# Neighbourhood attention: probabilities scaled on VectorE and plainly transposed, in place of products with a diagonal of 1/sum

## The reference, cut to what matters

```python
s = concatenate([s_nb + bias, s_cx], axis=-1)       # scores of one query
p = softmax(s.astype(float32), axis=-1)
o = einsum(p_nb, v_win) + einsum(p_cx, v_c)         # float32 throughout
```

## Time and profile before

| | us |
|---|---|
| executions | 4262.36, 4264.66, 4271.78 |
| median | 4264.66 |
| span of the profiled execution | 4259.6 |
| TensorE busy in the span | 3857.9 |
| VectorE busy | 1835.2 |
| ScalarE busy | 1324.2 |
| GpSimd busy | 456.7 |

### The profile page before, as it was taken

The page is one execution under the profiler, slowest core; times in us unless marked ns, Lnnn a source line. Parts: engine busy times, 40 slices in busy tenths (PEclk is TensorE's granted clock), DMA queues, the critical chain, the costliest instruction groups (busy, mean ns, idle before and its releaser), DMA issues.

```text
span 4259.6 us, 52528 instructions
## 1 busy us (share of the span) xinstructions
PE 3857.9 (91%) x21392; PEld 3013.5 (71%) x21392; DVE 1835.2 (43%) x2812; ACT 1324.2 (31%) x1963; POOL 456.7 (11%) x379
## 2 busy tenths in 40 slices
PE   7788878999998999899978889899998798989999
PEld 3555546788886787688865667678886566767887
DVE  2544443533334334444434354544333435454333
ACT  3332322322223323323333431233232333123222
POOL 0211110000002211000021230000011122000000
PEclk9878889999998999899989999999999999999999
DMA  4112243121111222232211221032321121113322
GB/s 162 53 48 80 90 170 108 50 70 60 60 53 57 80 95 85 74 102 92 89 46 34 68 57 40 30 106 90 99 85 41 43 74 50 33 39 108 96 93 69
DMA packets 320320, 317.03 MB, mean 74 GB/s; under 512 B 8720, under 2 KB 286128, under 8 KB 319952
## 3 DMA queue, kind: packets, MB, share of 16 engines
q1 hardware_dynamic: 320080, 313.67, 23.3%
HBM read 311.55 MB, written 2.10 MB: 74 GB/s over the span
## 4 chain that ended last, share of the span: by engine, by line
PE 78%; DVE 11%; ACT 5%; DMA 2%; issue 2%; POOL 1%; DVEq 0%; SPq 0%; ACTq 0%; POOLq 0%
PE PS L132 78%; DVE scr L146 5%; ACT scr L142 3%; DMA ring<-in_ada_w 1%; DVE scr L156 1%; DVE scr L164 1%; DVE PS L160 1%; ACT L142 1%; PE PS L135 1%; DVE NBt L156 1%; DVE scr L168 1%; POOL ring_r L146 1%; POOL NBt L146 0%; DVE scr L176 0%; DVE scr L152 0%
## 5 line engine op out<-in xcount | busy, mean ns | idle before, releaser
L132 PE MATMUL PS<-scr 128*32 128x32 f32 (+7 forms) x6692 | 648.1, 279 | 144.9 <-DVE scr L146 69.6
L132 PEld LDWEIGHTS PS<-scr 128*128 128x128 f32 (+4 forms) x6692 | 529.2, 167 | 291.2 <-issue 119.6
L132 PE MATMUL PS<-ffn_h,ffn_w 128*128 128x512 f32 (+1 forms) x3168 | 616.2, 357 | 7.8 <-DVE ffn_h L156 5.7
L132 PEld LDWEIGHTS PS<-ffn_h,ffn_w 128*128 128x128 f32 x3168 | 524.7, 190 | 100.5 <-issue 9.1
L142 ACT ACTIVATE scr<-PS 128x256 f32<-128x256 f32 (+5 forms) x425 | 193.2, 455 | 820.8 <-PE PS L132 752.6
L132 PE MATMUL PS<-h_h,ring_r 128*128 128x512 f32 (+1 forms) x976 | 356.6, 428 | 38.2 <-POOL ring_r L146 24.3
L142 ACT ACTIVATE scr<-scr 128x256 f32<-128x256 f32 (+7 forms) x404 | 212.6, 526 | 519.9 <-DVE scr L156 322.3
L132 PE MATMUL PS<-mlp_h,mlp_w 128*128 128x512 f32 x1536 | 361.3, 396 | 0.0
L132 PE MATMUL PS<-mlp_g,mlp_w 128*128 128x512 f32 x1536 | 359.7, 396 | 0.0
L132 PEld LDWEIGHTS PS<-mlp_h,mlp_w 128*128 128x128 f32 x1536 | 288.4, 188 | 70.5 <-issue 1.0
L132 PEld LDWEIGHTS PS<-mlp_g,mlp_w 128*128 128x128 f32 x1536 | 288.5, 188 | 69.9
(11 more groups left out here) (151 smaller groups left out, 4736.6 us busy)
## 6 DMA issues: line engine op xcount, KB each, us to landing
ring<-in_ada_w SPq DMA_DIRECT2D x48, 1024.0 KB, 6.1
ring<-in_ffn_w_in SPq DMA_DIRECT2D x44, 1024.0 KB, 5.0
ring<-in_w_up SPq DMA_DIRECT2D x32, 1024.0 KB, 5.5
ring<-in_w_down SPq DMA_DIRECT2D x32, 1024.0 KB, 5.0
ring<-in_w_in SPq DMA_DIRECT2D x60, 512.0 KB, 3.9
ring<-in_ffn_w_out SPq DMA_DIRECT2D x16, 1024.0 KB, 5.1
scr<-in_na_bias SPq DMA_DIRECT2D x32, 512.0 KB, 5.0
ring<-in_na_w_qkv SPq DMA_DIRECT2D x24, 512.0 KB, 4.2
```

The source lines that it names most:

```text
L132: return self.eng.matmul(o, lhsT=l, rhs=r, start=start, stop=stop) if self.eng else Nothing()
```

## The change

The diagonals go, and the buffer `dg` with them (the small buffers laid out behind it move up). VectorE takes the reciprocals of the sums as before and then scales `Pm` in place, one tensor-scalar operation of 128x512 per head, each with a count of its own. TensorE waits per head and transposes the four blocks of the head with the identity. The in-place scaling takes the place, on VectorE's queue, that the diagonal had: behind the reciprocal, ahead of the bias steps of the next item. The wait for the flip two items back, which protected `dg`, goes; ScalarE's own wait for that flip still protects `Pm`.

```diff
-    dg = [naa(256).rearrange("p (h t) -> p h t", h=2) for _ in range(2)]
@@ na_pe
         def flip(it):
             z = it % 2
-            pe.wait_ge(*at("n_dg", it))
             for hf in range(2):
+                pe.wait_ge(*at("n_sc", it, hf))
                 o = psum("n_pt", it, 1)[:, 512 * hf:512 * hf + 512]
                 for c in range(4):
-                    t = pe.mm(o[:, c * 128:c * 128 + 128], Pm[z][:, hf, c * 128:c * 128 + 128], dg[z][:, hf, :], True, True)
+                    t = pe.tr(o[:, c * 128:c * 128 + 128], Pm[z][:, hf, c * 128:c * 128 + 128], ident)
                 t.then_inc(*pe.up("nt_full", it, hf))
@@ na_dve
         def spread(it):
             z = it % 2
             dve.wait_ge(*at("n_ex", it))
-            dve.recip(nst[z][:, 4:6], nst[z][:, 4:6]).then_inc(*dve.up("n_dg"))
-            if it >= 2:
-                dve.wait_ge(*at("nt_full", it - 2, 1))
-            dve.tt(dg[z], bc(ident, 1, 2), bc(nst[z][:, 4:6], 2, 128), ALU.mult).then_inc(*dve.up("n_dg", it))
+            dve.recip(nst[z][:, 4:6], nst[z][:, 4:6]).then_inc(*dve.up("n_sc"))
+            for hf in range(2):
+                dve.ts(Pm[z][:, hf, :], Pm[z][:, hf, :], nst[z][:, 4 + hf:5 + hf], None, ALU.mult, None).then_inc(*dve.up("n_sc", it, hf))
```

## The result

Nine executions of the changed kernel have a median of 4288.93 us (4278.88 to 4291.16), nine of the kernel before 4264.66 (4258.28 to 4280.49). The ratio of executions taken side by side is 1.0037, with a 95% interval of 1.0025 to 1.0049: slower by 15.8 us (10.7 to 20.9) on 4264.66. The forecast was slower by 12.3.

A forecast was written before the change was run, and what follows sets the result against it. TensorE was taken to bound the stage, with one hole per head pair. +0.8 us without the clock, +8.5 for five clock falls and +3 for the last pair gave +12.3, so 4277.0 us; range 4256 to 4284.

The forecast's parts named there:

- What bounds it: The changed stage: TensorE bounds it, busy 191.88 of 200 us, with one hole in each head pair's fourth item.
- The transposes: TensorE's flip: 8 records instead of 16, 0.85 us saved in a pair's first two items, 0.53 in the third.
- The scalings: VectorE, per item: two scalings of 0.486 us replace a diagonal of 0.43, adding 0.58 us.
- The meeting with GpSimd: Fourth item: GpSimd's chunk starts 0.14 us before VectorE's first scaling and blocks it; next values start 1.90 us later.
- V: Start of the value products of a head pair's third item (m=2), from which later steps are timed.
- The sum without the clock: Whole stage: six pairs and the last pair +1.2 us each, pair 6 -1.65; total +0.8 us.
- The clock: TensorE's clock falls at the fourth item's hole, 2.96 us, since 2.69 us elsewhere brought a fall and 2.24 did not.
- The size of the clock's term: Five falls in six pairs, 1.7 us each, +8.5 us; the last pair at half clock +3.
- the double stretch: Upper bound of the clock's price: two slow stretches in a row, six times 3.4 us plus 5, +25 us.
- C: Rival: the clock does not fall; 4265.5 us with GpSimd first, 4259.8 with VectorE first; chance 0.22.
- B: Rival: VectorE's scaling starts before GpSimd's chunk and the clock falls; 4271 us; chance 0.16.
- D: Rival: scalings meet no GpSimd chunk and the clock holds; -10.3 us, 4254.3, near 4262 with some falls; chance 0.12.

The follow-up runs named there:

- e1: Changed kernel plus 20 identity transposes filling TensorE's hole in every pair's fourth item and the last pair; ratio to the kernel before 1.0006 (0.9995 to 1.0018).
- e2: Changed kernel with GpSimd's chunks cut from 512 to 2 columns for all pairs but the first; ratio to the kernel before 0.9979 (0.9968 to 0.9991).
- e3: Changed kernel with the two scalings done by ScalarE instead of VectorE; ratio to the kernel before 0.9999 (0.9983 to 1.0015).
- e4: Kernel before with plain transposes in place of the products, diagonal made but unused, division left out; ratio to the kernel before 0.9987 (0.9974 to 0.9999).
- e9: Kernel before with plain transposes, diagonal unused, division left out, plus 16 identity transposes filling the hole; ratio to the kernel before 0.9963 (0.9950 to 0.9977).
- e5: Changed kernel with the scalings on ScalarE plus 14 identity transposes filling the hole; ratio to the kernel before 0.9949 (0.9931 to 0.9967).
- e6: Changed kernel with GpSimd's chunks cut to 2 columns after the first pair, plus 20 filling transposes; ratio to the kernel before 0.9965 (0.9953 to 0.9977).

## Why the prediction was right, point by point

*What bounds it.* One hole per pair in TensorE's work, filled by VectorE's steps: right, and the hole is where all of it was decided.

*The transposes.* Eight records, 0.79 us to the next product; forecast 0.85 for the flip and a gain of 0.85 in m=0 and m=1. Measured from result copy to result copy with the clock held (e1): 14.12 against 14.99 and 11.50 against 12.41, a gain of 0.87 and 0.91; m=1 to m=2 7.23 against 7.79, 0.56 where 0.53 was forecast.

*The scalings.* 1.01 us for two without GpSimd: the row of another stage held, and so did its form. What the *VectorE: DVE Perf Modes* page of the Trainium skill (the errata section) gives by its table, an estimate of 0.33 us each, is 0.16 short.

*The meeting with GpSimd.* I had GpSimd first by 0.14 us; it was first by 0.12 (1528.22 and 1528.34), in this as in the other pairs of the kernel. The values of m=3 at V+8.75 was the forecast, V+8.72 the measurement. On the way there the count missed the 0.53 us before the bias step and had the negation 0.39 us too long; that both end with the fourth chunk is why the sum came out. The rule of the *SBUF — State Buffer* page of the Trainium skill (Who interferes with whom), the whole instruction for the one that comes first, holds in these rows: 2.85 us for two scalings, 5.43 for four chunks.

*The sum without the clock.* +0.8 us forecast. e1 is the changed kernel with the clock held: 298.4 against 297.5, +0.9. That the two agree so well is chance, for the items leave out the 0.9 us that the first flip gains, which the forecast has in. With it the sum measured is +0.1, 0.7 under the forecast. Its parts: six pairs 0.1 each (forecast 0.2), the copies from pair 5 to pair 6 -1.4 (39.52 against 40.94; -1.65), the last pair +1.0 (23.46 against 22.46; +1.2).

*The clock.* That it would fall was right, and so was the reason that it falls in this passage: TensorE's work there became shorter and the hole longer (3.10 us, forecast 2.96), and with the hole filled (e1) it doesn't fall. But the evidence that I drew it from was weaker than I wrote. I compared the hole with two others of the profile, 2.69 us with a fall and 2.24 without, as if the length of a hole decided. The same profile has one of 3.20 us without a fall (timeline, and the stretch behind it):

```profile
2727.24 0.50 PE L132 MATMUL PS<-h_h,mlp_w 128*128 128x512 f32 x1 [3.20 <-DVE mlp_w L146]
```

```profile
2727.00:2737.00 10.00, 9.76 (x42) 7.96 (x43) 8.28 (x5) 1.95 (x3) 0.00 (x0) 1.00 0.33 105
```

It has one of 1.98 us ahead of 3369.65 as well, with the clock at 0.50 over 3371.5 to 3374.3. By these rows "no fall" was as open as the fall, so that it fell six times in six was in part luck.

*The size of the clock's term.* It was sized too low: 11.5 us (five falls of 1.7 and 3 for the last pair) against 16.6 measured. Two steps of it were off. I took five falls in six pairs: it fell in each. And I took a stretch at 0.50 of 3.4 us, after the one row I had the earlier trace rows: in all of the six pairs but the first it was as long as the one shown, 6.7 us. Behind a hole a pair then lost 1.6 to 2.7 us (43.15 to 44.27 against 41.60). I had the double stretch only as a bound. The last pair lost 2.6 us (26.01 against 23.46), near the 3.

*The time.* 4277.0 was forecast; the ratio puts it at 4280.4 (4275.3 to 4285.6). The median of the nine executions, 4288.93, lies 4.9 us above the upper end of the range, 4284: of the 24.3 us between the medians 8.5 are not in the ratio, and no run here explains them. The 15.8 us that are in it exceed the forecast by 3.5. In the stage the clock's term alone was 5.1 us short and the rest 0.7 us too high; the difference lies within the interval of the ratio.

*The rivals.* C, no fall, is e1, and its 4265.5 would have been right for it (the ratio puts e1 at 4267.2, from 4262.5 to 4272.3). B did not occur; GpSimd was first. D was out twice: the scalings met the chunks, and the clock would have fallen without them (e2). Its price was off too: the 0.05 us per pair still had the blocked negation in it, and with small chunks the values of m=3 start at V+6.3 to V+6.7, where it had V+6.90.

Left open: what exactly makes the clock fall. In this stage holes of 2.29 (e3), 2.48 (e2) and 2.66 us (e4) did it, with shorter idle times ahead of each; 1.57 us (before) and 0.94 (e1) did not, and neither did 2.64 us in pair 0 of e3. Elsewhere in the kernel before 2.24 and 3.20 us did not, 1.98 and 2.69 us did. So the length of the last hole doesn't settle it, and no run varied the hole alone in small steps. What the runs do show is that filling this hole holds the clock, in four kernels of four.

## What to carry to other kernels

Time that is taken from the engine that bounds a stage, but next to a wait on another engine, does not vanish: it lengthens the idle time, and here that dropped TensorE's clock for the dense work behind it, so that shorter flips alone gained nothing in the stage (e4) and with the hole filled by idle work 13.7 us (e9, 0.4% of the kernel). Both leave the division out; e5, which has it, gained 0.5%. Read the granted clock of the stretch around every hole, and when an edit makes a hole longer, price the stretch behind it at both levels before you price the edit. Don't take the length of the hole as a test: look for every hole of like length in the profile, with and without a fall. And before a single-source float32 operation is put on VectorE, look at what GpSimd does at that moment: the same scaling took 0.5 or 1.4 us, and on ScalarE 0.7 whatever GpSimd did.

## What the runs showed of the hardware that was not expected

The clock fell after idle times of 2.3 us in five pairs of e3 and not after one of 2.64 us in its first pair, nor after 3.20 us elsewhere in the kernel before. In the pair shown of the changed kernel it came back only 6.7 us later, although TensorE had dense work from 1535.32 on, 1.5 us after the fall. Plain transposes of the identity, 14 to 20 of them in a hole, were enough to hold it at 1.00 (e1, e5, e6, e9). A small operation suffers from GpSimd like a large one: the negation of 128x2 took 0.17 us alone, 0.38 in the changed kernel and 1.11 in e3; the diagonal of 128x256 took 0.43 us and beside a chunk 0.85 (e4). GpSimd's chunks of 2 columns, four in 1.45 us, did not slow two scalings beside them (1.00 us).
